# Block two of a two-block kernel: x and the down projections with tokens on partitions, spread gate rows, a split output projection, unrolled layers

## The chip, the cores and the metric

One core of one Trainium2 chip runs the whole program. The metric is the device time of one execution in microseconds (us). The profile comes from one further execution.

## The reference

Two model blocks run one after the other on 256 tokens of width 1024, each with two layers; a root-mean-square norm stands between them. The change touches block two. In short:

```python
def swiglu(h, w_gate, w_up, w_down):
    return (jax.nn.silu(h @ w_gate) * (h @ w_up)) @ w_down      # D_FF = 2816

def second_block(x, c, ...):
    for l in range(DEPTH):                                      # DEPTH = 2
        mod = (silu(c) @ ada_w[l] + ada_b[l])[:, None, :]       # nine rows of 1024
        sh1, sc1, g1, sh2, sc2, g2, sh3, sc3, g3 = jnp.split(mod, 9, axis=-1)
        h = rmsnorm(x, norm_pre[l, 0]) * (1.0 + sc1) + sh1
        y = swiglu(h, ffn_w_gate[l, 0], ffn_w_up[l, 0], ffn_w_down[l, 0])
        x = x + 0.5 * g1 * rmsnorm(y, norm_post[l, 0])
        h = rmsnorm(x, norm_pre[l, 1]) * (1.0 + sc2) + sh2
        y = hybrid_mixer(h, ...)                                # two attentions of 8 heads each
        x = x + g2 * rmsnorm(y, norm_post[l, 1])
        h = rmsnorm(x, norm_pre[l, 2]) * (1.0 + sc3) + sh3
        y = swiglu(h, ffn_w_gate[l, 1], ffn_w_up[l, 1], ffn_w_down[l, 1])
        x = x + 0.5 * g3 * rmsnorm(y, norm_post[l, 2])
    return x

def hybrid_mixer(h, ...):                                       # its end
    y = concatenate([rmsnorm(ya, group_gain[:512]), rmsnorm(yb, group_gain[512:])], axis=-1)
    return y @ w_out
```

## The kernel before, in words

Each engine (TensorE `pe`, ScalarE `scalar`, VectorE `vector`, GpSimd `gpsimd`, SyncE `sync`) has its own program, written out by hand. Semaphores in `S` order them; every engine works strictly in the order of its program. SyncE issues all weight loads, through a ring of four buffers of 3 MB; a load waits in `acquire` until its buffer was given back with `release`.

In block two `x` and `h` lie transposed: the 1024 features on partitions in 8 slices `k`, the 256 tokens on the free axis. A feed-forward works through 11 units of 256 hidden columns. For exact f32 results each weight piece of 128x1024 is split in a high and a low part of a faster format: ScalarE writes the high part (`high`, line 1238), VectorE the low one (`low`, line 1598), into three slots `wsp`. TensorE multiplies `high*high`, `high*low` and `low*high` (`thrice`, lines 628 to 630), 96 products for gate and up (`gate_up`) and 48 for down (`down`), and gives a slot back through `S.wused`. In the first feed-forward of a layer (`f=0`) VectorE also computes one modulation piece per unit (`ada_unit`, line 1558), of which TensorE makes sums (`ada_sum`, line 615) and VectorE `mod` (`ada_mod`, line 1567). In the second (`f=1`) it does two pieces of the next layer.

Products in plain f32 (the mixer's projections, the attention, the output projection, all sums) appear as two records each in the profile.

A norm needs sums over features, which lie on partitions: ScalarE squares 8 slices (line 1189), TensorE adds them by products with a matrix of ones (`sum_squares`, line 607), ScalarE takes the root (line 1209), VectorE the reciprocal over all tokens (line 1581). `post` (line 1928) then scales the result, VectorE and GpSimd add it to `x` (lines 1933 and 2183), and the next norm begins with the same steps. The mixer's attention runs over 8 pairs of heads: `scores`, softmax, `turn_pair` (line 1097), a copy by VectorE, `value_pair` (lines 1110, 1111). Behind it stand the norms of the two head groups and the output projection (line 1163).

The two layers are one loop of the program (`Fori`), and `boundary` at its end drains all engines, clears the semaphores and lets them go on together; SyncE waits for it too.

Of the kernel before, what the change touches and what calls it, by code (L numbers as in the profile page):

```python
# [23 lines left out]
P = 128  # L24
# [7 lines left out]
POOL_ADDS = 5  # L32
X_ORDER = [0, 1, 2, 5, 3, 6, 7, 4]
# [67 lines left out]
def down_piece(e, j):  # L101
# [19 lines left out]
SCORE_BANK = [4, 4, 4, 4, 4, 0, 4, 0]  # L121
VALUE_BANK = [2, 2, 2, 2, 2, 3, 2, 3]
# [5 lines left out]
         "gt_t gt cs_t cs gathl whi wlo wused prod ph hl atl sil act at_t at yg sc_t xs xe mm qk vv S sc nm e p T pt pv y yn inv post xp xd dn gsel hth htl end").split()  # L128
# [9 lines left out]
def build(nc, a, out, scratch):  # L138
    with ExitStack() as ctx:
# [42 lines left out]
        none = sb("none", [P, 16])  # L182
# [57 lines left out]

        qa, at = carve(0, 4, T)
# [22 lines left out]
        act_own, dve_own, pool_own, pe_own = cleared[-4:]  # L264

# [101 lines left out]
        def _(sp):  # L367
# [22 lines left out]
            def ahead_unit(blk, l, u):  # L390

                unit = (AHEAD_1, AHEAD_2)[blk][u]
                cols = slice(u * COLS, (u + 1) * COLS)
                with sp.If(l < L - 1):
                    acquire(blk, l, unit)
                    after = nc.s_assert_within(l + 1, 1, L - 1, skip_runtime_bounds_check_because=
                                               "this way is taken only where l < L - 1")
                    ada_columns(unit, (a.w_ada, a.ada_w_2)[blk], after, cols)
                with sp.Else():
                    acquire(blk, l, unit)  # L400
                    if blk == 0:
                        ada_columns(unit, a.ada_w_2, 0, cols)
                    else:
                        sp.sem_inc(landed[unit % RING][0], 32)
                        sp.sem_inc(landed[unit % RING][1], 16)
# [70 lines left out]
            def next_rows(blk, l):  # L476

                with sp.If(l < L - 1):
                    sp.wait_ge(rows_read, l + L * blk + 1)
                    (rows_1, rows_2)[blk](nc.s_assert_within(l + 1, 1, L - 1, skip_runtime_bounds_check_because=  # L480
                                                             "this way is taken only where l < L - 1"))
                if blk == 0:
                    with sp.Else():
                        sp.wait_ge(rows_read, L)
                        rows_2(0)
# [22 lines left out]
            with sp.Fori(0, L) as l:  # L508
# [27 lines left out]
                ahead_unit(0, l, 0)  # L536
                ahead_unit(0, l, 1)
                group_unit(0, l, OUT_1[1], a.w_out, [3])
                ahead_unit(0, l, 2)
# [3 lines left out]
                next_rows(0, l)  # L543

            with sp.Fori(0, L) as l:
# [3 lines left out]
                sp.wait_ge(layer_go, l + L + 2)  # L549
                lc = bass.ds(l, 1)  # L550
# [20 lines left out]
                ahead_unit(1, l, 0)  # L571
                ffn_unit(l, 1, FFN_2B[0], 0)
                for u in range(1, AHEAD):
                    ahead_unit(1, l, u)
# [3 lines left out]
                for e in range(9, UNITS_FF):  # L578
                    if e == UNITS_FF - 1:
                        next_rows(1, l)  # L580
                    ffn_unit(l, 1, FFN_2B[e], e)
            sp.wait_ge(out_e, 4)
            otile = tA.rearrange("p k t -> p (k t)").rearrange("p (h d) -> p h d", h=TH)
            sp.dma_start(out[0].rearrange("(h p) d -> p h d", p=P), otile).then_inc(fin, 16)
            sp.wait_ge(fin, 16)
# [3 lines left out]
        def _(pe):  # L589
# [11 lines left out]
            def sum_squares(n, parts=1, bank=2, order=range(KD)):  # L601

                for i, k in enumerate(order):
                    pe.wait_ge(S.sq, 8 * n + i + 1)
                    half = k * parts // KD
                    per = KD // parts
                    last = mm(ps[:, bank, half * T:half * T + T], ones[:], tA[:, k, :],  # L607
                              start=(i % per == 0), stop=(i % per == per - 1))
# [10 lines left out]
            def vectors(n_a, n_b):  # L619
# [1606 lines left out]
```

## Time and profile before

| | |
|---|---|
| median of 3 runs | 2358.16 us (2356.41 to 2358.89) |
| the profiled execution | 2357.19 us, span 2355.4 us |
| granted TensorE clock, mean | 0.954 |
| TensorE busy | 2141.6 us, 91% of the span |
| VectorE busy | 1622.4 us, 69% |
| ScalarE busy | 1013.6 us, 43% |
| GpSimd busy | 83.8 us, 4% |
| loads | 543.40 MB, mean 231 GB/s |

The chain of work that ended last lies on TensorE for 75% of the span, on VectorE for 15%, on loads for 3%. Block one ends at about 1071 us, block two takes the rest. The clock is in shares of 2.4 GHz. A line number in a row is that of the kernel before.

### The profile page before, as it was taken

The numbers are of one execution on the slowest core, as the hardware profiler recorded it, in microseconds if no ns is written. First come the engines' busy times: TensorE is split into PE (matmuls) and PEld (weight loads), VectorE is DVE, ScalarE is ACT, GpSimd is POOL, SyncE is SP. The second block draws the span as 40 slices with busy tenths as digits, with TensorE's granted clock in tenths as the row PEclk, the third lists the DMA queues.
The fourth block names the chain that finished last, engine by engine and source line by source line (L and its number), as shares of the span: only waits on it lengthen the run. The fifth ranks groups of instructions, "written<-read, shape, count | busy, mean of one in ns | idle before, by whom it ended". The sixth has DMA issues, their size and how long they took to land.

```text
span 2355.4 us, 33193 instructions
## 1 busy us (share of the span) xinstructions
PE 2141.6 (91%) x12719; PEld 1900.4 (81%) x12719; DVE 1622.4 (69%) x2159; ACT 1013.6 (43%) x1458; POOL 83.8 (4%) x143
## 2 busy tenths in 40 slices
PE   4999899997998999996999897899969998978997
PEld 2788788886887888885999676799969996667997
DVE  5898799996987898994787434664458863437543
ACT  0121778774022877873433322344433342314443
POOL 0010000000100000000000010000000000100000
PEclk8999899998998999997999998899989999988999
DMA  7949598885668689883799412586248983024730
GB/s 274 338 158 342 235 373 343 336 333 197 237 247 333 235 338 373 340 321 113 259 334 317 143 37 90 214 286 197 72 154 307 339 278 108 19 93 142 242 113 18
DMA packets 252025, 543.40 MB, mean 231 GB/s; under 512 B 14291, under 2 KB 172525, under 8 KB 227309
## 3 DMA queue, kind: packets, MB, share of 16 engines
q1 hardware_dynamic: 251852, 541.50, 63.6%
q8 instruction: 89, 1.46, 0.3%
q14 instruction: 52, 0.42, 0.1%
q10 hardware_dynamic: 32, 0.02, 0.0%
HBM read 540.42 MB, written 1.07 MB: 230 GB/s over the span
## 4 chain that ended last, share of the span: by engine, by line
PE 75%; DVE 15%; DMA 3%; issue 3%; ACT 2%; SPq 1%; DVEq 0%; POOL 0%; ACTq 0%
PE ps L595 12%; PE ps L628 10%; PE ps L630 9%; PE ps L629 9%; PE ps L689 5%; PE ps L691 5%; PE ps L690 4%; PE ps L607 4%; DVE acc L1558 3%; DVE arena L1687 3%; PE ps L1163 3%; PE ps L729 2%; PE ps L731 2%; PE ps L730 2%; DVE ring_lo L1841 2%
## 5 line engine op out<-in xcount | busy, mean ns | idle before, releaser
L1841 DVE TENSOR_TENSOR ring_lo<-ring,wsg 128x1024 fp32r<-128x1024 f32 x384 | 459.8, 1224 | 45.7 <-ACT wsg L1286 38.8
L1598 DVE TENSOR_TENSOR wsp<-ring,wsp 128x1024 fp32r<-128x1024 f32 x264 | 321.8, 1224 | 212.0 <-ACT wsp L1238 204.9
L1286 ACT ACTIVATE wsg<-ring 128x1024 fp32r<-128x1024 f32 x384 | 405.8, 1059 | 81.7 <-PE ps L691 54.8
L628 PE MATMUL ps<-hsp,wsp 128*128 128x256 f32 x1408 | 407.3, 289 | 34.6 <-DVE hsp L1619 18.6
L1238 ACT ACTIVATE wsp<-ring 128x1024 fp32r<-128x1024 f32 x264 | 277.3, 1055 | 364.5 <-PE ps L630 321.4
L629 PE MATMUL ps<-hsp,wsp 128*128 128x256 f32 x1408 | 403.9, 287 | 0.0
L630 PE MATMUL ps<-hsp,wsp 128*128 128x256 f32 x1408 | 403.9, 287 | 0.0
L595 PE MATMUL ps<-arena,ring 128*128 128x256 f32 (+1 forms) x1760 | 379.4, 382 | 4.9 <-PE ps L595 4.2
L595 PEld LDWEIGHTS ps<-arena,ring 128*128 128x128 f32 (+1 forms) x1760 | 317.7, 184 | 58.8 <-issue 7.6
L628 PEld LDWEIGHTS ps<-hsp,wsp 128*128 128x128 f32 x1408 | 276.1, 196 | 38.0 <-DVE wsp L1598 22.5
L629 PEld LDWEIGHTS ps<-hsp,wsp 128*128 128x128 f32 x1408 | 276.0, 196 | 0.0
L630 PEld LDWEIGHTS ps<-hsp,wsp 128*128 128x128 f32 x1408 | 275.7, 196 | 0.0
L1558 DVE SCALAR_TENSOR_TENSOR acc<-ring,cvec,acc 128x768 f32<-128x768 f32 x217 | 221.0, 1018 | 10.1 <-DVE wsp L1598 3.6
L689 PE MATMUL ps<-wsg,hsg 128*128 128x512 f32 x512 | 207.6, 406 | 0.1
L628 PE MATMUL ps<-asp,wsp 128*128 128x256 f32 x704 | 201.5, 286 | 3.3 <-DVE wsp L1598 3.3
L691 PE MATMUL ps<-ring_lo,hsg 128*128 128x512 f32 x512 | 201.4, 393 | 0.0
L629 PE MATMUL ps<-asp,wsp 128*128 128x256 f32 x704 | 199.4, 283 | 0.0
L630 PE MATMUL ps<-asp,wsp 128*128 128x256 f32 x704 | 199.4, 283 | 0.0
L690 PE MATMUL ps<-wsg,hsg 128*128 128x512 f32 x512 | 199.4, 389 | 0.0
L607 PE MATMUL ps<-arena,ones 128*128 128x256 f32 x304 | 95.3, 482 | 50.9 <-ACT arena L1189 49.7
L628 PEld LDWEIGHTS ps<-asp,wsp 128*128 128x128 f32 x704 | 135.2, 192 | 6.5 <-DVE wsp L1598 6.5
L1687 DVE SCALAR_TENSOR_TENSOR arena<-arena,vec 128x256 f32<-128x256 f32 x240 | 129.3, 539 | 8.6
(219 smaller groups left out, 2781.2 us busy)
## 6 DMA issues: line engine op xcount, KB each, us to landing
ring<-in_w_expert_gate_dram SPq DMA_DIRECT2D x64, 1024.0 KB, 6.9
ring<-in_w_expert_up_dram SPq DMA_DIRECT2D x64, 1024.0 KB, 9.0
ring<-in_w_expert_down_dram SPq DMA_DIRECT2D x64, 1024.0 KB, 5.0
ring<-in_ada_w_dram SPq DMA_DIRECT2D x48, 1152.0 KB, 8.6
ring<-in_ffn_w_gate_dram SPq DMA_DIRECT2D x44, 1024.0 KB, 11.1
ring<-in_ffn_w_up_dram SPq DMA_DIRECT2D x44, 1024.0 KB, 13.2
ring<-in_ffn_w_down_dram SPq DMA_DIRECT2D x44, 1024.0 KB, 5.2
ring<-in_w_ada_dram SPq DMA_DIRECT2D x32, 1152.0 KB, 11.5
```

Source lines behind the costliest of these rows:

```text
L595: last = mm(dst, wk(k), rhs(k), start=(k == 0), stop=(k == n - 1))
L628: mm(dst, hi, v_hi, start=start, stop=False, skip_group_check=True)
L629: mm(dst, hi, v_lo, start=False, stop=False, skip_group_check=True)
L630: return mm(dst, lo, v_hi, start=False, stop=stop, skip_group_check=True)
L689: mm(dst, hi, w_hi, start=(k == 0), stop=False)
L690: mm(dst, lo, w_hi, start=False, stop=False)
L691: last = mm(dst, hi, w_lo, start=False, stop=(k == KD - 1))
L1238: act_(split_part(at % SPLITS, 0, n), piece(unit, n), ACT.Identity).then_inc(S.whi, 1)
L1286: act_(high_piece(n % HIGHS, j), piece(EXPERT_1[e], j), ACT.Identity).then_inc(S.whi, 1)
L1558: last = v_.scalar_tensor_tensor(acc[:, slot, :], w[:, k, :], cond[:, k:k + 1], acc[:, slot, :], ALU.mult, ALU.add)
L1598: v_.tensor_tensor(split_part(at % SPLITS, 1, n), piece(unit, n), split_part(at % SPLITS, 0, n, F32), ALU.subtract).then_inc(S.wlo, 1)
L1841: v_.tensor_tensor(low_piece(EXPERT_1[e], j), piece(EXPERT_1[e], j), high_piece(n % HIGHS, j, F32), ALU.subtract).then_inc(S.wlo, 1)
```

## The change

1. `x` is kept with tokens on partitions (`xt`). The down projections take the tokens as the stationary operand and 512 weight columns as the moving one, and their last unit runs quarter by quarter (`QUARTERS`, `S.yq`).
2. Mean squares over features come from ScalarE's running sum (`root_of`). TensorE turns `x` back by products with a diagonal of the reciprocal roots (`turn_x`, `scale_x`), which also scale it. Ahead of them stand 12 products into an unused bank (`keep_warm`).
3. The row gate x gain is spread over all partitions by TensorE (`gate_spread` on VectorE, `spread_gate` on TensorE, `keep_gate` on ScalarE).
4. The output projection is split by head group: `out_local` for the first group between the last pairs of the attention, `out_part(1, ...)` for the second; the groups' reciprocal roots are applied afterwards, on VectorE.
5. The layers are written out one after the other, with semaphores of their own for the attention. There is no boundary before, between or behind them, GpSimd no longer adds, the last layer leaves out the next layer's modulation, and the output is stored from `xt` in three pieces.

The core of the diff (names of semaphores, allocations and the attention's `S.` to `A.` left out):

```diff
             def down(at, count, slot, first, final):
-                for c in range(2):
-                    pe.wait_ge(S.wlo, count + c + 1)
-                    for d in range(KD):
-                        last = thrice(ps[:, 4 + d // 2, d % 2 * T:(d % 2 + 1) * T], (at + c) % SPLITS, 4 + c,
...
+                def products(c, hf, parts):
+                    hi, lo = (split_part((at + c) % SPLITS, part, 4 + c) for part in range(2))
+                    t_hi, t_lo = (asp[:, slot, part, c, hf * P:(hf + 1) * P] for part in range(2))
+                    for tok, w, start in ((t_hi, hi, first and c == 0), (t_hi, lo, False), (t_lo, hi, False)):
+                        for dh in parts:
+                            last = mm(yps(hf, dh), tok, w[:, wide_cols(dh)], start=start,
+                                      stop=(final and c == 1 and tok is t_lo), skip_group_check=True)
+                    return last
+                if not final:
+                    for c in range(2):
+                        pe.wait_ge(S.wlo, count + c + 1)
+                        for hf in range(TH):
+                            last = products(c, hf, (0, 1))
+                        last.then_inc(S.wused, 1)
+                    return
...
+            def keep_warm():
+                for _ in range(WARM):
+                    mm(ps[:, 0, 0:P], ones[:], ident[:], start=True, stop=True)
+            def turn_x(j):
+                for hf in range(TH):
+                    pe.wait_ge(S.dx, TH * j + hf + 1)
+                    for k in range(KD):
+                        last = mm(xT(k)[:, hf * P:(hf + 1) * P], xt[:, hf, k * P:(k + 1) * P], diag[:, hf, :],
...
+            def spread_gate(n, part, bank=2):
+                if part == 0:
+                    pe.wait_ge(S.dg, n + 1)
+                elif bank == 2:
+                    pe.wait_ge(S.gr, 2 * n + 1)
+                mm(ps[:, bank, :], ones[:], spread[:, wide_cols(part)], start=True, stop=True).then_inc(S.rep, 1)
...
+                    spread_gate(gate, 0)
                     pe.wait_ge(S.prod, base + 10)
                     gate_up(58, pb + 58)
...
+                    spread_gate(gate, 1)
                     dn(9, 62, pb + 62, base + 10)
...
+            def root_of(src, ready, sums, part, root, done):
+                def one(hf):
+                    for dh in range(2):
+                        ready(hf, dh)
+                        at = 2 * hf + dh
+                        own(act_(junk[:, hf, dh, :], src(hf, dh), ACT.Square, accum_out=sums[:, at:at + 1]))
...
+            def gate_spread(gate_at, factor, gain_at):
+                own.link(v_.scalar_tensor_tensor(gpost, mod[:, gate_at:gate_at + KD], factor,
+                                                 vA[:, gain_at:gain_at + KD], ALU.mult, ALU.mult))
+                v_.tensor_tensor(spread.rearrange("p (k q) -> p k q", k=KD),
+                                 ident[:].unsqueeze(1).to_broadcast([P, KD, P]),
+                                 gpost.unsqueeze(2).to_broadcast([P, KD, P]), ALU.mult).then_inc(S.dg, 1)
...
+            def add_row(j, hf, src, scale=True):
+                n = own.n
+                add(hf, src, 0, n - 1)
+                if hf and scale:
+                    scale_x(j, 0)
+                add(hf, src, 1, n)
+                if hf and scale:
+                    scale_x(j, 1)
...
+                    for q in range(3):
+                        both_groups(q)
+                    eng.wait_ge(S.gr, 2 * j0 + 4)
+                    post(j0 + 2, 0, mine, atok)
+                    both_groups(3)
+                    add_row(j0 + 2, 0, atok)
+                    eng.wait_ge(A.yc, 4)
+                    post(j0 + 2, 1, mine, atok)
+                    add_row(j0 + 2, 1, atok)
```

`both_groups(q)` waits for quarter `q` of the second group, gives back the output weights' buffers at quarters 1 and 3, and adds the two groups; `post` multiplies by reciprocal root and gate row.

VectorE at the end of the loop over units in the first feed-forward. `wsp<-ring,wsp` is a low part, `mod<-ps,vec` a modulation piece; before:

```order
L1567 TENSOR_TENSOR mod<-ps,vec 128x6
L1992 REGISTER_ALU
L1992 COMPARE_AND_BRANCH
L1598 TENSOR_TENSOR wsp<-ring,wsp 128x1024 x3
L1607 TENSOR_TENSOR silu<-silu,ps 128x512
```

and now:

```order
L1714 TENSOR_TENSOR mod<-ps,vec 128x6
L2176 REGISTER_ALU
L2176 COMPARE_AND_BRANCH
L2051 SCALAR_TENSOR_TENSOR std<-mod,vec 128x8
L2053 TENSOR_TENSOR arena<-ident,std 128x1024
L1744 TENSOR_TENSOR wsp<-ring,wsp 128x1024 x3
```

The two operations of `gate_spread` (L2051, L2053) now stand between the loop and the last three low parts before the product.

TensorE at the same place, now. L694 are the down products of unit 8, L653 the modulation's sums, L667 the first product of `gate_up(58)`:

```order
L694 MATMUL ps<-wsp,asp 128x512 x12
L653 MATMUL ps<-ones,acc 128x1 x6
L1086 REGISTER_ALU
L1086 COMPARE_AND_BRANCH
L1064 MATMUL ps<-arena,ones 128x512
L667 MATMUL ps<-hsp,wsp 128x256
```

The spread product (L1064) is new, ahead of the next unit's products.

TensorE at the end of the attention, from the turn of pair 5 on (L1097 or L1184: a turn; L1110, L1111 or L1196, L1197: values), before:

```order
L1097 MATMUL ps<-ident,arena 128x128 x6
L1110 MATMUL ps<-pt,arena 64x256
L1111 MATMUL ps<-pt,arena 64x128
L1110 MATMUL ps<-pt,arena 64x256
L1111 MATMUL ps<-pt,arena 64x128
L607 MATMUL ps<-arena,ones 128x256 x8
L1163 MATMUL ps<-arena,ring 128x256 x48
```

and now:

```order
L1184 MATMUL ps<-ident,arena 128x128 x6
L1225 MATMUL ps<-ring,arena 128x256 x4
L1196 MATMUL ps<-pt,arena 64x256
L1197 MATMUL ps<-pt,arena 64x128
L1196 MATMUL ps<-pt,arena 64x256
L1197 MATMUL ps<-pt,arena 64x128
L1225 MATMUL ps<-ring,arena 128x256 x4
L1222 MATMUL ps<-ring,arena 128x512 x4
L1207 MATMUL ps<-ones,arena 128x1 x8
```

The last pair is shown in both. Parts of the projection (L1222, L1225) now stand between a turn and its values, and the block of eight sums over 256 columns (L607) has gone.

## Rows read from the trace of the kernel before

**Rows 1.** Busy us (count) per engine, granted clock, share and GB/s of DMA, per stretch.

```profile
core 0: us, PE busy (x) PEld busy (x) DVE busy (x) ACT busy (x) POOL busy (x), PEclk, DMA share, GB/s
1425.00:1450.00 25.00, 16.28 (x69) 12.31 (x69) 8.20 (x10) 5.52 (x14) 1.61 (x2) 0.70 0.00 0
1476.00:1480.00 4.00, 3.79 (x18) 3.00 (x16) 0.00 (x0) 0.17 (x1) 0.00 (x0) 1.00 1.03 402
...
1850.00:1875.00 25.00, 25.00 (x208) 24.67 (x207) 21.07 (x23) 9.19 (x12) 0.00 (x0) 1.00 0.92 313
```

**Rows 2.** Timeline of TensorE: start, us, operation; block one, steady down products, the mixer.

```profile
504.39 0.39 PE L729 MATMUL ps<-wsg,act_r 128*128 128x512 f32 x1
...
506.89 0.39 PE L731 MATMUL ps<-ring_lo,act_r 128*128 128x512 f32 x1
...
1299.84 0.28 PE L629 MATMUL ps<-asp,wsp 128*128 128x256 f32 x1
...
1307.52 0.28 PE L630 MATMUL ps<-asp,wsp 128*128 128x256 f32 x1
...
1406.00 7.03 PE L595 MATMUL ps<-ring,arena 128*128 128x512 f32 x16
```

**Rows 3.** Timeline from the last down product to the mixer, layer 0.

```profile
1307.64 3.62 PE L607 MATMUL ps<-arena,ones 128*128 128x256 f32 x16
...
1311.87 1.75 DVE L1581 RECIPROCAL std<-std 128x256 f32<-128x256 f32 x1 [5.02 <-ACT std L1209]
...
1321.44 1.75 DVE L1581 RECIPROCAL std<-std 128x256 f32<-128x256 f32 x1 [2.88 <-ACT std L1209]
...
1324.53 2.99 PE L1047 MATMUL ps<-arena,ring 128*64 128x256 f32 x13 [3.63 <-ACT arena L1225]
```

**Rows 4.** Timeline of TensorE: last values, and the sums behind the output projection.

```profile
1437.37 0.40 PE L1111 MATMUL ps<-pt,arena 128*64 128x128 f32 x4
...
1480.09 3.69 PE L607 MATMUL ps<-arena,ones 128*128 128x256 f32 x16 [0.31 <-PE ps L1163]
```

**Rows 5.** TensorE's waits, 1326 to 1449: us in total, times, longest.

```profile
PE ps L1110 <- DVE pt L2076: 5.4, 4, 2.3
```

**Rows 6.** Timeline: behind block one, the first products of three feed-forwards, a layer's end.

```profile
1072.43 1.28 ACT L1217 ACT_TABLE_LOAD   x1 [6.20 <-DVEq L315]
...
1100.05 0.55 PE L628 MATMUL ps<-hsp,wsp 128*128 128x256 f32 x1 [5.16 <-DVE hsp L1619]
...
1498.44 0.55 PE L628 MATMUL ps<-hsp,wsp 128*128 128x256 f32 x1 [4.16 <-DVE hsp L1619]
...
1703.46 3.62 PE L607 MATMUL ps<-arena,ones 128*128 128x256 f32 x16
...
1731.56 0.55 PE L628 MATMUL ps<-hsp,wsp 128*128 128x256 f32 x1 [5.16 <-DVE hsp L1619]
```

**Rows 7.** Timeline at the end of the program.

```profile
2334.86 3.62 PE L607 MATMUL ps<-arena,ones 128*128 128x256 f32 x16
...
2351.02 0.39 SPq L584 DMA_DIRECT2D out_dram<-arena  x1
```

**Rows 8.** Groups by line and shape from 1200 on: busy us, mean ns, idle before.

```profile
L1558 DVE SCALAR_TENSOR_TENSOR acc<-ring,cvec,acc 128x768 f32<-128x768 f32 x101 | 102.8, 1018 | 5.3 <-DVE wsp L1598 2.7
...
L1243 ACT ACTIVATE silu<-ps 128x512 f32<-128x512 f32 x39 | 23.3, 597 | 71.0 <-PE ps L630 71.0
...
L2047 DVE SCALAR_TENSOR_TENSOR arena<-ps,bias 128x512 f32<-128x512 f32 x16 | 11.0, 688 | 38.6 <-PE ps L1085 38.6
```

**Rows 9.** Timeline around the end of unit 8's down products, f=0 and f=1.

```profile
1283.27 1.40 PE L615 MATMUL ps<-ones,acc 128*128 128x1 f32 x12
...
1285.88 0.16 DVE L1567 TENSOR_TENSOR mod<-ps,vec 128x6 f32 x1
...
1677.95 1.06 ACT L1238 ACTIVATE wsp<-ring 128x1024 fp32r<-128x1024 f32 x1 [1.82 <-PE ps L630]
...
1679.04 1.23 DVE L1598 TENSOR_TENSOR wsp<-ring,wsp 128x1024 fp32r<-128x1024 f32 x1 [1.66 <-ACT wsp L1238]
```

**Rows 10.** TensorE's waits in layer 1's second feed-forward, 2125 to 2335.

```profile
PE ps L628 <- DVE wsp L1598: 5.8, 4, 2.4
```

More of the change, by code:

```diff
@@ L264, in build @@
         act_own, dve_own, pool_own, pe_own = cleared[-4:]
+        attention = [Named(**{n: sem(f"{n}_{l}") for n in ATTENTION}) for l in range(L)]
         block = ctx.enter_context(nc.Block())
@@ L599, in hk, with sum_squares @@
                 return h[:, k, :]
[L601 to L608, printed above, removed]
+            def sum_squares(n, bank):
+                for k in range(KD):
+                    pe.wait_ge(S.sq, 8 * n + k + 1)
+                    last = mm(ps[:, bank, 0:T], ones[:], tA[:, k, :], start=(k == 0), stop=(k == KD - 1))
                 last.then_inc(S.sum, 1)
@@ L1400, in _ @@
                 boundary(eng, own, l + 1)
-            table(ACT.Sqrt)
-            squares(xk)
-            root(0)
-            boundary(eng, own, L + 1)
-            with eng.Fori(0, L) as l:
-                squares(xk)
-                root(0)
-                table(ACT.Silu)
+            def root_of(src, ready, sums, part, root, done):
+                def one(hf):
+                    for dh in range(2):
+                        ready(hf, dh)
+                        at = 2 * hf + dh
+                        own(act_(junk[:, hf, dh, :], src(hf, dh), ACT.Square, accum_out=sums[:, at:at + 1]))
+                        own.wait()
+                        if dh == 0:
+                            own(act_(part[:, hf:hf + 1], sums[:, at:at + 1], ACT.Identity, bias=eps[:, 0:1],
+                                     scale=1.0 / D))
+                    own.wait()
+                    act_(root[:, hf:hf + 1], sums[:, at:at + 1], ACT.Sqrt, bias=part[:, hf:hf + 1], scale=1.0 / D
+                         ).then_inc(done, 1)
+                return one
@@ L1411, in _, with both, keep_gate @@
+            def both(one):
+                for hf in range(TH):
+                    one(hf)
+            def keep_gate(n, part, bank=2):
+                eng.wait_ge(S.rep, 2 * n + part + 1)
+                act_(gate_row[:, wide_cols(part)], ps[:, bank, :], ACT.Identity).then_inc(S.gr, 1)
+            table(ACT.Sqrt)
+            both(root_y(0))
+            for l in range(L):
+                A = attention[l]
                 for f in range(2):
-                    base, pb, units = UNITS_FF * f, PIECES_FF * f, (FFN_2A, FFN_2B)[f]
+                    F, j0, gate = 2 * l + f, 3 * l + 2 * f, 3 * l + 2 * f
+                    base, pb, units = UNITS_FF * F, PIECES_FF * F, (FFN_2A, FFN_2B)[f]
```

706 lines of the change are left out of this document (411 added, 295 removed).

## The prediction

> **What bounds the kernel now.** First the busy time per stretch [rows 1]. In the feed-forward stretches (1850 to 1875) TensorE is busy for all 25 us, while VectorE has 21 us of work and the DMA engines 92%. At the end of attention (1425 to 1450) it is busy for 16 us, at a granted clock of 0.70. So the kernel has two parts: long stretches paced by TensorE's products, and seams in which one short operation waits for the next. Then the timeline of the pace. The down products of 256 columns start 64 steps apart between 1299.84 and 1307.52, so 0.120 us each; block one's products of 512 columns take 11 steps from 504.39 to 506.89, 0.227 each; a plain f32 product of 512 columns is two records, 16 in 7.03 us, 0.88 a product [rows 2]. Then the seams, in order of time [rows 3 to 6]. From its first feed-forward product to its last down product layer 0 takes 1100.05 to 1703.46, 603.4 us, and layer 1, the second pass of the same loop body, 1731.56 to 2334.86, 603.3 [rows 6, 7]. So a first pass through code costs nothing here, and unrolling the layers adds no term.
>
> **Part 1, pace of the down projection.** A unit of 256 hidden columns has 48 down products of 256 columns, 5.76 us. It gets 24 of 512 columns, stationary tokens, which is the shape of block one: 24 x 0.227 = 5.45. Gain 0.3 x 44 units = **-13**.
> The Trainium skill (TensorE: Matmul & The Clock Gate, "Wait — 56ns, not 53.3ns?") gives a warm product its columns at 2.4 GHz and about 2.5 ns more. By it both forms would cost nearly the same and this term would be -3; the trace's 13 ns above the columns for each product disagrees, and I use the trace.
>
> **Part 2, the final sums are no longer made on TensorE.** Today, from the last down product to the first product of the mixer: 8 squares summed by 16 records (3.6 us), root, a reciprocal of 256 columns (1.75), 8 multiplies, additions (POOL too), squares, 16 records, another 1.75, 8 multiplies, shift; 1307.64 to 1324.53, 16.9 us [rows 3]. With tokens on partitions the mean is one ACT operation with a running sum (512 columns from PSUM 0.60 [rows 8]; read-out and root 0.2 each, an estimate by the smallest operation shown, 0.16 [rows 9]). The chain behind the last product: ACT 1.2; a reciprocal of one column 0.2 and two multiplies of 512 columns at 0.69, 1.6; two additions, priced alike, with a diagonal (0.4) between, 1.8; ACT 1.1; reciprocal and diagonal 0.5; four of the eight turning products, 1.0; ACT writes h, 0.5. Sum 7.7, with semaphores 8.2. Twice: **-17.4**. The 24 warming records (2.9 us) lie in this wait and cost nothing; if the chain were shorter than 2.9 they would.
>
> **Part 3, end of attention.** Today the values end at 1437.8, then come group sums, reciprocal, gains and 64 projection products until 1480.09: 42.3 us [rows 4]. The projection is split by head group. Its first half (16 products at 0.88, 14.1 us) is put between values, and the means become 2 x 8 one-column products (16 records at 0.1, 1.65 us each). In the tail TensorE waits 5.4 us for the copied scores, in four waits [rows 5], and part of its turns run at half clock [rows 1]. With the filler TensorE has no long wait there. Laid out record by record at full clock the tail ends 4.3 us later, then come 14.1 + 1.65. So 42.3 becomes 20.0: **-44.6** for two layers. The bounds are nothing hidden (+14.1 for 4.3, each) and all of it hidden (-4.3).
>
> **Part 4, behind the projection.** Today 1480.09 to 1498.44, 18.4 us [rows 4, 6]. The new chain has one more multiply-add and one more turn and `low_tokens`: 9.7 in layer 1. In layer 0 VectorE first does five next-layer multiply-adds (1.02 each [rows 8]), before `both_groups(0)`, and stands 3 us late: 12.6. Together **-14.5**.
>
> **Part 5, layer boundary, start and end.** Boundary: 1703.46 to 1731.56, 28.1 us [rows 6], with a drain, block sums and vectors. It becomes part 2's chain with `low_tokens`, 9: **-19**. Start: from ACT's first operation after block one, 1072.43, to 1100.05, 27.6 [rows 6]. New: 16 turns (3.4, a one-column record takes 0.1 at full clock [rows 9], twice that at half), vectors and copies 0.9, four multiplies and two reciprocals 3.2, ACT 1.1, diagonal 0.5, 24 records between 2.9 (full clock) and 5.8 (half), I take 5, h and its low part 1.5: 15.6, **-12**. End: 2334.86 to 2355.4, 20.5 [rows 7]. New: part 2's chain to the last addition, 4.6, and a last 256 KB store; the 1 MB store of today took 4.4 from issue, I take 2.7: 7.3, **-13**. Stores, turns back and the boundary's drain are gone.
>
> **Part 6, what is added: the gate rows.** Four times in the feed-forward and twice in attention a row of gate x gain is spread over partitions by two f32 products, 2 x 0.88. That is **+7.0** in feed-forward, +3.5 in attention. But the first one stands in TensorE's order directly behind down 8, with `gate_up(58)` queued behind it, and waits for `dg`, which VectorE gives only after low part 60. In part f=1 that low part ends at 1680.27, 2.3 us after down 8 (ACT's high part starts when that ends, 1677.95) [rows 9]. Then comes the 8-column product 0.2 and the 1024-column one, priced as the low part's 1.23 (the nearest of that length): dg at 1681.8, a stop of 3.8 us. In f=0 the modulation of 1285.88 is last, dg at 1287.6, against the end of TensorE's 12 sum records, 1284.7: 2.9. Sum 2 x (3.8 + 2.9) = **+13.4**. All of `gate_up(58)` waits behind it, and nothing makes that up, since TensorE paces.
>
> **Part 7, layer 1's dummy work.** The loop computed a next-layer modulation in the last layer too. Unrolled, it is left out: 12-record sums, 3 x 1.24, -3.7, and the 5.8 us that TensorE waits for low parts behind VectorE's adaptions in its f=1 [rows 10] -5.8. **-9.5.**
>
> **Part 8, weights in layer 0, f=1.** Today unit 30's load goes out when half of the projection's products are done, over 30 us ahead of use. Now `both_groups(1)` frees its slot just 14 us ahead of use. Four loads of 3.1 MB (30, two ahead units, and gate and up of 33) stand before the second `gate_up`. At 402 GB/s [rows 1] that is 29 us from the release; use is 26 us behind it, and high, low and nine small row loads are in between. **+8** (0 to 13). The queue is SP's, in order, and layer 1 has no ahead loads there.
> The Trainium skill (DMA: Bandwidth & Descriptors, "Where 436 GB/s comes from") puts a core's share of HBM at about 358 GB/s. By it these loads would take 32 us and this term would be +12; the measured 402 speaks for my value.
>
> **Part 9, clock.** Behind a seam TensorE starts at the lower level of 1.2 GHz (0.55 us for the first product, against 0.28 in the steady stretch [rows 2, 6]). Warming saves perhaps 1 us at each of five places; a stop of 3.8 us at dg can lower the clock again, 1 us at each of four. **-1** (-6 to +7).
>
> **Sum.** -13 -17.4 -44.6 -14.5 -19 -12 -13 +7 +3.5 +13.4 -9.5 +8 -1 = **-112**. The profiled execution took 2357.2 (span 2355.4 and 1.8 around it), 1 below the median of 2358.2. So 2357.2 - 112 = 2245, and 2246 against the median.
>
> **The rivals.**
> *A, the seams hardly shorten (chance 0.17).* ACT and VectorE now hand over about eight times per seam, and what I put at 0.05 to 0.1 may be 0.3; attention's filler may push the values back rather than fill waits. Against it: today's handovers are short: the sum ends at 1311.26, the reciprocal starts at 1311.87 [rows 3], and a root lies between. Six seams x 3, half projection unhidden 2 x 9.8, DMA stop 13 in place of 8: 2245 + 18 + 20 + 5 = 2288.
> *B, it goes better (0.14).* No clock loss, dg stop shorter since down 8 is quicker than ACT's chain, DMA stop hidden, tail of attention wholly hidden: 2245 - 5 - 4 - 8 - 8 = 2220.
> *C, slower (0.03).* Moving weights in the split format do not keep block one's pace when four PSUM banks are written in turn. From 0.333 us a product on, (0.333 - 0.227) x 1056 = 112, all is lost; at the 0.44 of an f32 record it would be 2245 + 225 = 2470. Block one's own down, from 504.39, writes two banks in turn and keeps 0.227.
> *My forecast (0.66)*, own range 2232 to 2262.
>
> **How the numbers follow.** 2246 is the likeliest. For eight in ten the range takes in most of B and the near half of A: 2222 to 2280. A measurement of this kernel can tell about 0.2% (5 us) from no change. Faster: forecast, A and B hold 0.97, of which I leave 0.01 to no change; slower is C, 0.03. Loads in f=0 are no rival of weight: 92% busy today, and a unit that keeps its length there gives back 7 of the 112 at most.
>
> **What would show it.** Right: 24 down records at 0.227 apart; a stop of 2.5 to 4 us before each first spread product; 8 to 10 us from last down product to the mixer's first; no wait over 1 us between value 4 and 7; about 20 us from the last value of today's kind to the end of projection; in layer 0 an f=1 longer than layer 1's by 15 us. Wrong: down products above 0.24 apart, gate_up at half clock for more than 4 us behind a dg stop, projection products in the tail that wait for `oev` or `y`, or loads late in f=0.

## The result, and the profile after

The kernel after takes **2259.23 us** (median of 4 runs, 2258.86 to 2260.46), beside 2357.45 before in the same comparison: ratio 0.9584, 95% interval 0.9567 to 0.9600. That is 98 us less, where 112 were forecast; the time of 2246 was forecast with a range of 2222 to 2280. The profiled execution took 2259.53, span 2257.8, granted clock 0.969 on average.

The page of after: the span, TensorE's busy time, the granted clock in 40 slices, and the shares of the chain that ended last.

```profile
span 2257.8 us, 31008 instructions
PE 2102.1 (93%) x11747; PEld 1809.7 (80%) x11747; DVE 1586.0 (70%) x2135; ACT 1025.4 (45%) x1505; POOL 61.9 (3%) x113
...
PEclk7999899999899899999999999999999999999999
...
PE 68%; DVE 17%; DMA 5%; issue 4%; ACT 3%; SPq 2%; DVEq 0%; POOL 0%; ACTq 0%; PEldq 0%
```

TensorE is busy for 39.5 us less than before (2141.6), so more than half of the gain is time in which it stood. The seams are in its timeline (start, us, operation, in brackets the idle time before it and who ended it). L1046 are the warming products, L1053 turns `x`, L667 is the first gate product, L1135 the mixer's first, L1225 the last of the projection.

```profile
1077.43 3.18 PE L1046 MATMUL ps<-ident,ones 128*128 128x128 f32 x24
1082.43 3.99 PE L1053 MATMUL ps<-std,x 128*128 128x128 f32 x32 [1.82 <-DVE std L2061]
1087.23 0.35 PE L667 MATMUL ps<-hsp,wsp 128*128 128x256 f32 x1 [0.81 <-DVE hsp L2145]
...
1298.82 2.92 PE L1046 MATMUL ps<-ident,ones 128*128 128x128 f32 x24
1303.25 2.05 PE L1053 MATMUL ps<-std,x 128*128 128x128 f32 x16 [1.51 <-DVE std L2061]
1305.52 2.05 PE L1053 MATMUL ps<-std,x 128*128 128x128 f32 x16 [0.21 <-DVE std L2061]
1307.50 1.35 PE L1135 MATMUL ps<-arena,ring 128*64 128x256 f32 x4
...
1441.43 0.59 PE L1225 MATMUL ps<-ring,arena 128*128 128x256 f32 x2
1441.87 2.84 PE L1046 MATMUL ps<-ident,ones 128*128 128x128 f32 x24
1452.43 5.94 PE L1053 MATMUL ps<-std,x 128*128 128x128 f32 x32 [7.72 <-DVE std L2061]
1459.19 0.36 PE L667 MATMUL ps<-hsp,wsp 128*128 128x256 f32 x1 [0.82 <-DVE hsp L2145]
...
1674.52 2.92 PE L1046 MATMUL ps<-ident,ones 128*128 128x128 f32 x24 [0.15 <-PE ps L694]
1684.08 0.36 PE L667 MATMUL ps<-hsp,wsp 128*128 128x256 f32 x1 [0.81 <-DVE hsp L2145]
...
2038.71 2.84 PE L1046 MATMUL ps<-ident,ones 128*128 128x128 f32 x24
2045.07 6.55 PE L1053 MATMUL ps<-std,x 128*128 128x128 f32 x32 [3.52 <-DVE std L2061]
2052.27 0.36 PE L667 MATMUL ps<-hsp,wsp 128*128 128x256 f32 x1 [0.66 <-DVE hsp L2145]
...
2239.40 11.52 PE L694 MATMUL ps<-wsp,asp 128*128 128x512 f32 x48
```

The reader is to see two things. Behind a down projection the seam is 8.7 us (1298.82 to 1307.50), in place of 16.9 [rows 3], and the turning products run at full clock, 16 records in 2.05. Behind the output projection TensorE stands for 7.72 and 3.52 us, and then 32 records take 5.94 and 6.55 us, not 4.1.

TensorE's waits in block two (in total, times, longest):

```profile
PE ps L1053 <- DVE std L2061: 18.2, 9, 7.7
PE ps L1064 <- DVE arena L2053: 12.8, 4, 3.7
PE ps L667 <- DVE wsp L1744: 12.4, 10, 2.4
PE ps L667 <- DVE silu L1753: 6.9, 4, 2.6
```

From such starts the whole difference of the two spans comes out place by place. For layer 1 of before I take layer 0's stretches, since both took the same time [rows 6, 7]. "Forecast" is made of the prediction's parts.

| stretch | before, us | after, us | forecast | measured |
|---|---|---|---|---|
| block one, to ScalarE's first operation behind it (1073.74) | 1072.4 | 1073.7 | 0 | +1.3 |
| from there to the first gate product | 27.6 | 13.5 | -12 | -14.1 |
| f=0, each layer | 207.6 | 211.6 | +1.4 | +4.0 |
| last down product to the mixer, each layer | 16.9 | 8.7 | -8.7 | -8.2 |
| mixer to the projection's end, each layer | 155.6 | 134.4 | -20.6 | -21.2 |
| projection to the first gate product, layer 0 | 18.4 | 17.3 | -5.8 | -1.1 |
| the same, layer 1 | 18.4 | 13.6 | -8.7 | -4.8 |
| f=1, layer 0 | 205.0 | 215.3 | +10.3 | +10.3 |
| f=1, layer 1 | 205.0 | 198.7 | -7.2 | -6.3 |
| layer boundary | 28.1 | 9.6 | -19 | -18.5 |
| last down product to the end | 20.5 | 6.9 | -13 | -13.6 |

With "each layer" counted twice this is -97.6, the difference of the spans. The forecast's sum, with its -1 for the clock, is -112.

### The profile page after: what moved, and what is told of

Same layout as the page of the kernel before. It is cut to its first block, busy times and chain, and to the rows that moved or that the text cites. A ratio compares the mean times of both kernels' runs of the same rounds, so it can differ in the third digit from the quotient of the medians.

```text
span 2257.8 us, 31008 instructions
## 1 busy us (share of the span) xinstructions
PE 2102.1 (93%) x11747; PEld 1809.7 (80%) x11747; DVE 1586.0 (70%) x2135; ACT 1025.4 (45%) x1505; POOL 61.9 (3%) x113
## 4 chain that ended last, share of the span: by engine, by line
PE 68%; DVE 17%; DMA 5%; issue 4%; ACT 3%; SPq 2%; DVEq 0%; POOL 0%; ACTq 0%; PEldq 0%
PE ps L636 13%; PE ps L694 7%; DVE acc L1705 6%; PE ps L667 5%; PE ps L669 5%; PE ps L668 5%; PE ps L740 5%; PE ps L742 5%; PE ps L741 5%; DVE arena L1825 3%; DVE wsp L1744 3%; DMA ring<-in_ffn_w_up_dram 2%; PE ps L780 2%; PE ps L782 2%; PE ps L781 2%
## 5 line engine op out<-in xcount | busy, mean ns | idle before, releaser
L1340 ACT ACTIVATE wsp<-ring 128x1024 fp32r<-128x1024 f32 x264 | 277.5, 1056 | 377.7 <-PE ps L669 274.9
L667 PE MATMUL ps<-hsp,wsp 128*128 128x256 f32 x1408 | 407.5, 289 | 22.3 <-DVE wsp L1744 12.4
L667 PEld LDWEIGHTS ps<-hsp,wsp 128*128 128x128 f32 x1408 | 273.6, 194 | 28.0 <-DVE wsp L1744 14.4
L694 PE MATMUL ps<-wsp,asp 128*128 128x512 f32 x1056 | 255.9, 396 | 3.3 <-DVE wsp L1744 1.8
L694 PEld LDWEIGHTS ps<-wsp,asp 128*128 128x128 f32 x1056 | 195.5, 189 | 51.6 <-DVE wsp L1744 10.4
L742 PEld LDWEIGHTS ps<-ring_lo,hsg 128*128 128x128 f32 x512 | 96.0, 188 | 21.6
L740 PEld LDWEIGHTS ps<-wsg,hsg 128*128 128x128 f32 x512 | 96.8, 189 | 18.5 <-DVE ring_lo L1979 1.0
L741 PEld LDWEIGHTS ps<-wsg,hsg 128*128 128x128 f32 x512 | 96.5, 188 | 18.5
## 6 DMA issues: line engine op xcount, KB each, us to landing
ring<-in_ffn_w_up_dram SPq DMA_DIRECT2D x44, 1024.0 KB, 13.6
```

The lines of the kernel that those rows point to most:

```text
L667: mm(dst, hi, v_hi, start=start, stop=False, skip_group_check=True)
L694: last = mm(yps(hf, dh), tok, w[:, wide_cols(dh)], start=start, stop=(final and c == 1 and tok is t_lo), skip_group_check=True)
L740: mm(dst, hi, w_hi, start=(k == 0), stop=False)
L741: mm(dst, lo, w_hi, start=False, stop=False)
L742: last = mm(dst, hi, w_lo, start=False, stop=(k == KD - 1))
```

## The experiments

All are edits of the kernel after. Block one is the same in all of them, and yet the first gate product of block two starts anywhere from 1083.4 to 1090.8 us. So effects of a few us are read from stretches of block two in the trace, and the medians alone decide only the large ones.

| run | median, us | against after | ratio to before |
|---|---|---|---|
| e1_spread_later | 2256.51 | -2.7 | 0.9569 (0.9553 to 0.9585) |
| e2_down_256 | 2269.79 | +10.6 | 0.9629 (0.9613 to 0.9645) |
| e3_light_loads | 2255.19 | -4.0 | 0.9573 (0.9556 to 0.9590) |
| e4_local_after | 2282.85 | +23.6 | 0.9683 (0.9667 to 0.9699) |
| e5_barrier | 2266.01 | +6.8 | 0.9613 (0.9598 to 0.9628) |
| e6_high_behind_root | 2258.71 | -0.5 | 0.9575 (0.9562 to 0.9589) |
| e7_no_warm | 2267.51 | +8.3 | 0.9615 (0.9602 to 0.9628) |
| e8_more_warm | 2257.96 | -1.3 | 0.9574 (0.9561 to 0.9587) |
| e9_spread_and_copy_later | 2241.71 | -17.5 | 0.9506 (0.9493 to 0.9519) |
| e10_adaption_3_3_2 | 2259.27 | 0.0 | 0.9589 (0.9574 to 0.9605) |
| e11_together | 2238.45 | -20.8 | 0.9488 (0.9475 to 0.9501) |
| e12_together_rows_later | 2234.48 | -24.8 | 0.9470 (0.9457 to 0.9483) |

### The stop for dg: e1 and e9

`dg` is VectorE's signal that the gate row may be spread. e1 moves the spread products and ScalarE's copies of them one step later.

```diff
-                    spread_gate(gate, 0)
                     pe.wait_ge(S.prod, base + 10)
                     gate_up(58, pb + 58)
+                    spread_gate(gate, 0)
...
-                    spread_gate(gate, 1)
                     dn(9, 62, pb + 62, base + 10)
+                    spread_gate(gate, 1)
...
-                    keep_gate(gate, 0)
                     hi(62, 9, 4)
                     hi(63, 9, 5)
                     gate_silu((base + 10) % 2, pb + 62)
-                    keep_gate(gate, 1)
+                    keep_gate(gate, 0)
                     hi(64, 10, 4)
                     high_act((base + 10) % 2, base + 11, pb + 58)
+                    keep_gate(gate, 1)
                     hi(65, 10, 5)
```

> The four spread products of the feed-forward parts stand one chunk later in TensorE's order (part 0 behind gate_up(58), part 1 behind down 9), and ACT copies them later. Theory (the stop for dg is a real cost): the four waits of 2.6, 3.7, 2.7 and 3.7 us vanish, and with them the half-clock stretch behind each (about 2 us): 2259 - 12.8 - 6 = 2240. Rival (the stop only fills slack, since VectorE's low parts and ACT's copies pace the last two units): the waits go over to the low parts 61 to 65 or to the copied gate row, and the time stays at 2256 to 2261.

The four waits for `dg` were gone, but only 2.7 us came back. By the median alone the rival would have won. The trace of e1 says otherwise: first ScalarE's row, then TensorE's.

```profile
1292.33 0.60 ACT L1541 ACTIVATE arena<-ps 128x512 f32<-128x512 f32 x1 [4.26 <-PE ps L1064]
1292.82 1.05 ACT L1340 ACTIVATE wsp<-ring 128x1024 fp32r<-128x1024 f32 x1
```

```profile
1291.27 1.02 PE L1064 MATMUL ps<-arena,ones 128*128 128x512 f32 x2
1295.28 2.06 PE L694 MATMUL ps<-wsp,asp 128*128 128x512 f32 x8 [2.98 <-DVE wsp L1744]
```

My edit had put ScalarE's second copy of the gate row (L1541) ahead of its last high part (L1340). The copy stood 4.26 us for TensorE's spread product, the high part behind it, and TensorE for that: 3.0 us in three of the four places (in layer 0's f=1 it was 1.8, not the 3.0 that e9's expectation says). So the stop was moved, not removed. In e9 the line `keep_gate(gate, 1)` stands behind `hi(65, 10, 5)`, nothing else differs from e1.

> As e1, but ACT copies the second half of the gate row behind its last high part, not ahead of it (in e1 that high part stood 4.26 us behind the second spread product, and TensorE then waited 3.0 us for the last low part, four times). Theory (the stop for dg is a real cost of about 13 us, and e1 only moved it): 2256.5 - 4 x 2.5 = 2246 to 2249. Rival (ACT and VectorE pace the last two units in any order): 2255 to 2258, with the wait in another place.

2241.71 us, 4 us below the range I gave. The theory holds and the rival falls. In the trace the four stretches from unit 8's down to the last down product are, in order of time, 4.3, 4.6, 4.4 and 5.6 us shorter than in after, 18.9 in all (the rest of the profiled execution is 2.5 us longer). The waits for `dg` are 12.8 of these. The other 6.2 (1.7, 0.8, 1.7 and 1.9) go with the clock, which in after is lower behind each stop; the 0.8 is what is left in layer 0's f=1 beside a new wait of 0.7 us. Stretches of TensorE in after (busy us, granted clock, DMA share, GB/s), then in e9:

```profile
1266.00:1270.00 4.00, 4.00 (x24) 1.00 0.73 254
1270.00:1274.00 4.00, 1.39 (x4) 0.82 1.09 363
1274.00:1278.00 4.00, 4.00 (x25) 0.76 1.10 348
1278.00:1282.00 4.00, 4.00 (x36) 1.00 0.28 87
```

```profile
1270.00:1274.00 4.00, 4.00 (x33) 1.00 1.04 398
1274.00:1278.00 4.00, 4.00 (x36) 1.00 1.10 348
```

### The pace: e2 and e10

e2 splits each down product of 512 columns in two of 256.

```diff
-                            last = mm(yps(hf, dh), tok, w[:, wide_cols(dh)], start=start,
+                            for s in range(2):
+                                last = mm(yps(hf, dh)[:, s * T:(s + 1) * T], tok,
+                                          w[:, dh * 512 + s * T:dh * 512 + (s + 1) * T], start=start and s == 0,
```

> Each down product of 512 columns is split into two of 256, tokens still stationary, nothing else. Theory (the width of the product sets the pace): 48 products at 0.120 in place of 24 at 0.227, +0.3 us for each of the f=1 units, and in the f=0 units less, because there a weight load paces: 22 x 0.3 + 22 x 0.1 = +8 to 9, so 2268; +13 if all 44 units pay. Rival (the pace came from the other operand order, not from the width): no change, 2259.

+10.6 us: the f=1 units take 17.28 us (1519.34 to 1536.62) in place of 16.98, as before the change, 6.6 us over 22 units. The width sets the pace, not which operand is stationary. In f=0 the period moves by 0.1 only (18.83 for 18.74). Why, the trace of after shows in one unit of each kind: TensorE, weight loads, VectorE.

```profile
1150.35 6.06 PE L694 MATMUL ps<-wsp,asp 128*128 128x512 f32 x24
1156.25 0.28 PE L653 MATMUL ps<-ones,acc 128*128 128x1 f32 x2
...
1515.44 5.63 PE L694 MATMUL ps<-wsp,asp 128*128 128x512 f32 x24
1520.91 0.28 PE L667 MATMUL ps<-hsp,wsp 128*128 128x256 f32 x1
...
1153.35 2.63 PEld L694 LDWEIGHTS ps<-wsp,asp 128*128 128x128 f32 x12 [0.52 <-DVE wsp L1744]
...
1148.62 3.12 DVE L1705 SCALAR_TENSOR_TENSOR acc<-ring,cvec,acc 128x768 f32<-128x768 f32 x3
1152.07 1.23 DVE L1744 TENSOR_TENSOR wsp<-ring,wsp 128x1024 fp32r<-128x1024 f32 x1 [0.33 <-DVE acc L1705]
```

The same 24 products take 5.47 us in f=1 and 5.90 in f=0. Half way through, the weight load waits for a low part that VectorE gives at 1153.30, because three modulation multiply-adds stood ahead of it. The faster down reaches that point earlier, so 0.17 of the 0.30 us are kept (period 18.91 before, 18.74 after). e10 changes the split of those multiply-adds.

```diff
-                            ada_now(0, 2, j, i)
+                            ada_now(0, 3, j, i)
                             lo(13 + 6 * j, 2 + j, 3, i)
-                            ada_now(2, 5, j, i)
+                            ada_now(3, 6, j, i)
                             lo(14 + 6 * j, 1 + j, 4, i)
-                            ada_now(5, KD, j, i)
+                            ada_now(6, KD, j, i)
```

> In f=0 VectorE does the eight modulation multiply-adds of a unit as 3, 3 and 2 between its low parts, in place of 2, 3 and 3, so that the low part of the second down piece stands behind two of them and not three. Theory (that low part, at 1152.07 to 1153.30, is what TensorE's second half of the down waits for, 0.43 us in each f=0 unit): the f=0 period falls from 18.74 to 18.3 us in 20 units, 2259 - 8 = 2251. Rival (in f=0 the period is set by loads or by the 12 sum records): no change, 2257 to 2261.

The median did not move. In the trace the down of such a unit takes 5.47 us (1149.63 to 1155.10), and the period is 18.3 to 18.6, but only in five of seven cases, 18.8 to 18.9 in the others; the mean is 18.51, 1 to 1.1 us less per f=0 stretch. What that gave was taken back in the attention, whose code is the same: from the mixer's first product to the projection's end it took 136.05 and 136.09 us, 1.7 more than in after. All of it lies in one block of 32 records, here in e10 and then in after, with the granted clock of e10 in 2 us of it:

```profile
1346.84 8.86 PE L636 MATMUL ps<-arena,ring 128*128 128x256 f32 x32
1348.00:1350.00 2.00, 2.00 (x6) 0.50 0.00 0
```

```profile
1348.48 7.17 PE L636 MATMUL ps<-arena,ring 128*128 128x256 f32 x32
```

In the 26 attention passes of after and the twelve runs this block takes either 7.17 us (18 times) or 8.86 us: twice in e2 and e10, once in e3, e4, e5 and e6. No edit touches it, and what decides between the two is open. So a difference of a few us between two runs can come from this block alone.

In e12, on top of e11, the same edit gave 2.3 and 1.8 us (216.0 to 213.7, 215.2 to 213.4 from one seam to the next). There the block took 7.17 us. So the mechanism is real, a quarter to a half of the size I gave it, and what holds the remaining units at 18.8 is open.

### The loads: e3 and e12

```diff
                 for i, (k0, k1) in enumerate(THIRDS):
+                    k1 = k0 + 1 if part else k1
...
-                        last = v_.scalar_tensor_tensor(acc[:, slot, :], w[:, k, :], cond[:, k:k + 1],
+                        last = v_.scalar_tensor_tensor(acc[:, slot, :], w[:, (k if blk == 0 else 3 * (k // 3)), :], cond[:, k:k + 1],
```

> Block two's modulation loads fetch only one row in three of their weights (3 of 8 rows of 128 partitions), and VectorE multiplies these rows again in place of the others: the modulation is computed from wrong weights, with the same instructions on every engine. Theory (the DMA paces the f=0 units, and delays layer 0's f=1): the f=0 unit period falls from 18.8 to 18.4 us, 20 units, -7, and layer 0's f=1 loses its waits for low parts and the wait of 1.8 in a down, -6: 2246. Rival (VectorE's own adaptions and handovers pace both): same period, 2257 to 2260.

Half and half. In f=0 the DMA engines' share fell from 0.94 to 0.67 and the period stayed at 18.7: the loads do not pace f=0, and my theory falls there (VectorE does, above). In layer 0's f=1 5.5 us came back (224.9 to 219.4 us from its first gate product to that of the next layer). What the loads cost there is one row of ScalarE in after:

```profile
1473.32 2.00 ACT L1340 ACTIVATE wsp<-ring 128x1024 fp32r<-128x1024 f32 x2 [6.15 <-DMA ring<-in_ffn_w_up_dram]
1475.23 0.58 ACT L1345 ACTIVATE silu<-ps 128x512 f32<-128x512 f32 x1
```

The silu of unit 0 is queued behind high parts of unit 33, whose load is late. TensorE waits 2.63 us for its product (1477.42) and goes on at 0.21 us a product, not 0.12, for some 3 us. e12 issues the nine small row loads late, to get unit 33 out 4 us earlier:

```diff
-                if l < L - 1:
-                    sp.wait_ge(rows_read, L + l + 1)
-                    rows_2(l + 1)
                 with sp.Fori(0, 2) as i:
...
+                if l < L - 1:
+                    sp.wait_ge(rows_read, L + l + 1)
+                    rows_2(l + 1)
                 for e in range(9, UNITS_FF):
```

> e11, and VectorE's 3, 3, 2 of e10, and the nine small row loads for layer 1 issued behind eight more feed-forward units in layer 0's f=1, not ahead of unit 33. Theory (these row loads delay unit 33 by 4 us of issue time, and TensorE stands at 1473 to 1477 for it and then runs at half clock): layer 0's f=1 shortens by 2 to 4 us, f=0 by 2: 2238 - 5 = 2233. Rival (unit 33 waits for bytes, 12.6 MB at about 400 GB/s, and not for its place in the queue): f=1 keeps its 215 us, 2236 to 2238.

The rival holds for the row loads: layer 0's f=1 took 220.2 us against 219.9 in e11, and ScalarE stood 6.20 us for the same load. Unit 33's gate load was issued 15.0 us behind unit 30's, not 18.8, and yet the high parts that wait for it start 33.8 us behind the issue of unit 30's load in both runs. Bytes are late, not the place in the queue. All of e12's gain over e11 is in f=0.

### The filler in the attention: e4

All `out_local` calls stand as one block behind the last `value_pair`, `keep_local` behind `result(7)`:

```diff
-                    out_local(0, 0, 2)
                     token_sums(0)
                     value_pair(4)
-                    out_local(0, 2, 4)
...
                     value_pair(7)
-                    out_local(3, 2, 4)
+                    for q in range(4):
+                        out_local(q, 0, 4)
```

> The first half of the output projection isn't put between the values but stands as a block behind the last one, and ACT copies it there. Theory (the filler lies in waits of 4.3 to 5.4 us per layer and in half-clock stretches): the values end 10 us earlier per layer, the projection takes 14.1 us more: +4 to +10 per layer, 2259 + 8 to 20 = 2273. Rival (the filler only pushed the values back): 2259 to 2263.

+23.6 us, above the range I gave. Without the filler the last values end 117.9 us behind the mixer's first product (1310.58 to 1428.47), with it 117.1 (1307.50 to 1424.55). But 1.7 of the 117.9 are the slow block of e10, which came here in layer 0; in layer 1, where it did not, the two are 116.4 and 117.1. So over 13 of the 14.1 us of filler are hidden. The same last third of the attention in e4, then in after:

```profile
1390.00:1428.40 38.40, 30.98 (x177) 0.85 0.23 83
```

```profile
1387.00:1424.60 37.60, 37.15 (x214) 1.00 0.23 85
```

Without filler TensorE is busy for 31 of 38 us at a clock of 0.85; with it, for nearly all of the time at full clock. The filler takes the place of 7 us of standing and of the slow clock.

### Barrier, warming and the seam behind the projection: e5 to e8, e11

e5 adds at the head of layer 1, on TensorE, VectorE and GpSimd (on ScalarE behind its roots of `x`):

```diff
+                if l:
+                    eng.drain().then_inc(arrived, 1)
+                    eng.wait_ge(arrived, (L + 2) * 4)
```

> The four compute engines drain and meet before layer 1's first feed-forward part (ACT behind its roots of x), nothing else. The change took a barrier away and shortened the chain at the same place, 28.1 to 9.6 us. Theory (the gain of 18.5 came from the chain: no sums, no second reciprocal, no turns): the barrier alone costs 1 to 3 us, 2261. Rival (the barrier was the larger part): +8 or more, 2267.

The stretch over the boundary took 231.3 us against 224.9, +6.4: between the two theories. TensorE's rows divide it:

```profile
1677.36 4.93 PE L1046 MATMUL ps<-ident,ones 128*128 128x128 f32 x24 [6.88 <-DVEq L2113]
1682.13 3.74 PE L1053 MATMUL ps<-std,x 128*128 128x128 f32 x32
```

VectorE's last diagonal starts at 1676.97, and TensorE could turn from there. 4.77 us go to the warming products, which the barrier pushes from a wait onto the path. So a barrier costs under 2 us here, which leaves some 16 of the 18.5 for the shorter chain. Whether the drain inside the old loop cost the same was not tried.

e7 calls no warming products at all, e8 calls more in f=1, and e6 moves one line of ScalarE:

```diff
-                    keep_warm()
+                    keep_warm((40, 28)[l] if f else 12)
                     turn_x(j0)
```

```diff
-                    hi(0, 0, 0)
+                    if not f:
+                        hi(0, 0, 0)
                     both(root_x(j0))
+                    if f:
+                        hi(0, 0, 0)
```

> No warming products in block two. Theory (they keep the clock up in the seams): the turning products and the first gate products behind each of the six seams run at the lower clock, 2 to 3 us each, +12: 2271. Rival (they lie in a wait and change nothing, since the clock falls anyway as in the seam behind the projection): 2257 to 2260.

+8.3, two thirds of what I expected. Without warming the turning in layer 0's seam before the mixer takes 5.39 us (1306.24 to 1311.63) against 4.25. The stretches that end in seams behind a down grew by 1.2, 4.4 and 3.2 us (1.7 of the 4.4 is a longer wait for unit 33's load, 4.32 us against 2.63); those that end behind the projection shrank by 0.8 and 0.4, so there 12 warming products bought nothing.

> In f=1 alone 40 (layer 0) and 28 (layer 1) warming products in place of 12, so that they fill most of the wait of 7.7 and 3.5 us before the turning products. Theory (the 32 turning records of 5.94 and 6.55 us ran at half clock because TensorE had stood): turning falls to about 4 us and the gate products behind start at full clock, -2.5 each, 2254. Rival (the clock is held down by something else, such as the f32 products ahead): 2259, or later if the warming itself becomes the last thing to end.

> In f=1 ACT's first high part stands behind the two roots of x, not ahead of them. Theory (layer 0's roots stood 2.7 us behind a weight load that lands late): the seam behind the projection shortens by 2 to 3 us in layer 0 and by 0 to 1 in layer 1, so 2256. Rival (the late load is needed by the first gate product anyway, through high and low part, so the wait only moves): 2259, with the wait at the low part.

Neither median moves beyond its uncertainty, and the stretches show why. In layer 1 (mixer to first gate product, 148.0 us) more warming gives 145.5 and the later high part 145.8. In layer 0 more warming gives nothing (151.8 against 151.7): a wait of 2.0 us is left behind it, and turning still takes 5.47 us. The later high part gives 4.0 us in the seam (13.3 for 17.3; 149.4 from mixer to gate product, with e10's slow block in it) and takes 3.7 in f=1 (228.6 against 224.9), where the wait of 2.63 us becomes 6.82: the late load is needed anyway. In after, ScalarE's row in layer 0's seam:

```profile
1448.86 1.06 ACT L1340 ACTIVATE wsp<-ring 128x1024 fp32r<-128x1024 f32 x1 [2.72 <-DMA ring<-in_ffn_w_up_dram]
```

It stands ahead of the roots of `x`, and VectorE then waits 3.42 us for the first of them. e11 is e9 with both edits in layer 1 alone.

> e9's order of the spread and the copies, and in layer 1's f=1 alone both ACT's first high part behind the roots of x (e6) and 28 warming products (e8). Theory (the rest of the miss in layer 1's seam behind the projection is a weight operation ahead of the roots and turning at half clock): that seam falls from 13.6 to 9 to 10 us, and 2241.7 - 4 = 2238. Rival (the two don't add, since more warming then ends later than the roots): 11 us, 2239 to 2242.

```profile
2025.84 6.42 PE L1046 MATMUL ps<-ident,ones 128*128 128x128 f32 x56
2032.10 3.74 PE L1053 MATMUL ps<-std,x 128*128 128x128 f32 x32
2036.65 0.36 PE L667 MATMUL ps<-hsp,wsp 128*128 128x256 f32 x1 [0.82 <-DVE hsp L2148]
```

The seam is 10.8 us, not 13.6. Turning takes 4.55, not 7.20 with its handovers; the first diagonal is ready at 2031.06, 1 us before the warming ends, so a part of what was won goes to the warming, as the rival said. The version with all edits, e12, is 24.8 us below after, 5.3% below before.

## Why the prediction was right, and where it was off

- **Part 1, pace (-13): right mechanism, size off in f=0.** 0.30 per unit in f=1, shown by e2; about 0.17 in f=0, where a low part of VectorE is what the down waits for. That makes -10 to -11. By the rule of the Trainium skill that the prediction set against it the term would have been -3, and e2 would have cost 3; its 22 units of f=1 alone cost 6.6, and the trace holds.
- **Part 2 (-17.4): right**, -16.4.
- **Part 3 (-44.6, with 3.5 of part 6): right in size, -42.4 against -41.1, by a different division.** I hid 9.8 of 14.1 us; e4 shows that over 13 are hidden. What took it back is an attention that is longer by itself: 116.4 us without filler (e4, layer 1) against 113.2 before. 1.7 of these are the spread products; the rest was not taken apart.
- **Part 4 (-14.5): the step that was missed most, -5.9.** "9.7 in layer 1" took turning at full clock and nothing ahead of the roots of `x`; "stands 3 us late" in layer 0 named VectorE's multiply-adds. They ended at 1438.95, and what was late was the high part that waits for its load until 1448.86. e6, e8 and e11 show both causes in layer 1, where the seam takes 10.8 with both changed, against 9.7 forecast. In layer 0 e6 shows that moving the high part only shifts the wait for the load.
- **Part 5 (-19, -12, -13): right**, -18.5, -14.1, -13.6. e5 shows a barrier at this place as the small share; the old one was not tried.
- **Part 6, the dg stop (+13.4): right**, 2.61, 3.74, 2.67 and 3.74 us, 12.8 in all, and e9 gives back them and the clock.
- **Part 7 (-9.5): agrees.** Layer 1's f=1 changed by -6.3; with pace -3.3, stop +3.7, spread products +1.8 and 1.9 for the clock that leaves -10.4 for it. It was not tried alone.
- **Part 8 (+8): right mechanism, nearer 6.** Layer 0's f=1 came out 10.3 longer, as forecast, but partly by luck: about 1.9 of it is the clock behind the stop, which the forecast had in part 9. e3 gives back 5.5 with five eighths of the modulation bytes left out. The working was also off: four loads of 3.1 MB at 402 GB/s take 30.8 us, not 29. In after it was 33.9 from the issue of unit 30's load (1439.47) to the high parts that wait for unit 33's, at 399 to 405 GB/s from 1450 to 1462 and 344 to 382 from there to 1474; and the seam was longer, so that first use came 19.7 us behind the issue, not 14.
- **Part 9, clock (-1): each term too small.** It set 5 us saved by warming against 4 lost at the stops. The warming saves up to 8.3 (e7), the stops lose 6.2 (e9). Half-clock turning behind the projection, which it had at nothing, takes 4.3 (5.94 + 6.55 against twice 4.1) and is part of what part 4 missed.

Of the 14.6 us that the sum was short, 8.6 are part 4 and 5.2 are the two f=0 stretches, about 1.3 of pace and 1.7 of clock in each, less 0.3 for a shorter stop. The signs that it named held: stops of 2.6 to 3.7 us, seams of 8.7, no wait above 0.5 us between values 4 and 7, an f=1 that is 16.6 us longer in layer 0. Rival A (2288) priced the same kind of handovers too high; its unhidden projection did not happen. Of rival B only the hidden tail came. Rival C did not happen: the down products, with four banks written in turn, keep 5.47 us for 24.

## What to carry to other kernels

An instruction that waits should be read with the queue behind it: the 0.6 us copy of a gate row cost 3 us three times, and a weight operation ahead of a root cost 2.2 us in layer 1 (e6, 148.0 to 145.8), only by their place. When an edit removes a wait and the time stays, look in the trace whether the edit made the next one, before the wait is called harmless. And filler between dependent steps pays twice: it uses the standing time and keeps TensorE's clock up.

## What was not expected of the hardware

- A stop of TensorE of 2.6 us between long busy stretches lowers the granted clock to 0.82 and 0.76 in the two stretches of 4 us around and behind it. Behind a stop of 7.7 us it is 0.50, the lower level of 1.2 GHz, for a whole stretch of turning products. In the seams behind a down, where warming leaves a wait of 1.5 us, it stays 1.00. Both as stretches of after, the seam behind a down first:

```profile
1304.00:1308.00 4.00, 3.79 (x30) 1.00 0.01 4
```

```profile
1452.00:1456.00 4.00, 3.57 (x16) 0.50 1.04 404
```

- Products that only keep the clock up paid where a wait of 1.5 us or none was left (e7, e11). They did nothing where TensorE then stood for 7.7 us, nor in e8's layer 0, where 80 records left a wait of 2.0 us and the clock of the two stretches of 4 us from 1452 on was 0.83 and 0.74.
- The granted clock also fell to 0.50 with no stop of TensorE: in the slow block of e10, behind the modulation's 12 one-column records and eight of the scores. It cost 1.7 us in 8 of 26 passes of the same code.
- A switch of ScalarE's table takes 1.28 us in the trace: in the seam of layer 0 the operation ahead of it ends at 1304.95, the load starts at 1304.96 and the next operation, on one column, at 1306.25. The Trainium skill (ScalarE: Activation LUTs, "What ACT_TABLE_LOAD costs") puts a drain of about 1.38 us on top, 2.66 in all; the trace does not show it here.
- A running sum of ScalarE over 512 columns ends with a read-out of its own, 0.19 us, about what the prediction estimated for it.
